# Neighbourhood attention of the first block: the eight turns of a head pair for both heads together, with the next pair's projection chunks between them, and a product with a diagonal in place of scale and transpose

## The chip, the core and the metric

The kernel runs on one core of a Trainium2 chip. The metric is the device time of one execution in microseconds. Engines: PE is TensorE (matmul; PEld its weight loads), DVE is VectorE, ACT is ScalarE, POOL is GpSimd, SP issues most DMAs. Each engine runs its own instructions in order, and they meet at semaphores.

## What is computed

Two transformer blocks on 1024 tokens of 1024 channels in float32. The change is in the first block's mixer: a gated convolution and an attention over eight heads of 64 channels, both from one projection.

```python
z = rms_norm(x, norm1_g) @ w_in                # GLU halves, then q, k, v
conv_out = silu(layer_norm(depthwise_conv31(a * sigmoid(gate)) + bias))
q = rms_norm(q per head, q_norm_g); k = rms_norm(k per head, k_norm_g)
# tokens lie on a 16 x 64 grid; a query sees 8 rows x 16 columns round it
s = q . k * 64**-0.5 + rpb[...]                # per head
attn = softmax(s) @ v
x = x + concat(conv_out, attn) @ w_out         # then the feed-forward and block two
```

## The kernel before

Activations lie with channels on the 128 partitions and tokens along the free dimension. Each large product is made of **units** of 128 output channels: eight **chunks** (one for each 128 input channels) of six matmuls of 512 columns. Inputs and weights are each split in a high and a low fp32r part, and three products (high by high, low by high, high by low) for two halves of the tokens make the six. SP streams a unit's weights to `weight_raw` (two slots), POOL splits them (L386, L388), PE multiplies (`chunk`, L460; matmuls at L465), and DVE takes the result out of PSUM with the per-token scale.

The attention goes over four **pairs** of heads (c = 0 to 3). For each pair PE first makes three units q, k, v. DVE takes them out (L1410, L1412), and q and k are normalised per head: squares on ACT (L1003), a mean per head as a matmul (L488, `head_sum`), a first guess of the inverse root as Ln and Exp on ACT (L937, L939, behind a table load, L933), one refinement and the scaling on DVE (L1319 to L1326, L1422), and the split in high and low (ACT, L1426). Then v is turned by eight transposes (L594) and sixteen **half turns** follow, one head h and one block j of 128 queries each (`na_turn`). In the half turn n PE issues in order:

- `scores(n + 2)` (L559): three matmuls of 384 columns (256 in the first and last block), on 64 partitions, for the head's two or three key blocks;
- `values(n - 1)` (L581): the turned weights times v, one float32 matmul of 128 columns for each key block. A float32 matmul stands as two records;
- `turn(n)` (L572): one transpose of 128 columns for each key block.

DVE adds the bias table to the scores and finds the maximum (L1441), ACT takes the exponent with its sum (L1034), DVE the reciprocal (L1450), ACT multiplies by it (L1041), PE transposes, ACT copies to `probs_t` (L917). DVE also works on the 124 **taps** of the depthwise convolution, one pass over 1024 columns each (L1372, `conv`), some of them between the other steps: one follows each reciprocal. With c = 3 the taps are over, and the LayerNorm of the convolution is done between the steps (L1455 to L1507), with SiLU at the eleventh half turn (L1051). Then the output projection begins (L611); its first unit waits for each mix chunk's split (`mix_hi`, `mix_lo`).

The order of everything is written out by hand, engine by engine.

## Time and profile before

| | us |
|---|---|
| median of 3 runs | 2814.89 |
| lowest, highest | 2813.39, 2815.87 |
| the profiled execution | 2817.12 |
| its span, first to last instruction | 2815.1 |

The profiled execution is 2.2 us above the median, and 2.0 us of it lie outside the span. The span is read as stretches of time: the units of the first gated part end near 119.5 us, the four pairs lie between there and 529.5 us, where the output projection begins, and all that follows is untouched by the change. "Granted clock" is TensorE's, as a share of full speed (2.4 GHz); it is at 1.00 or 0.50, and a mean over a stretch can be in between.

### The profile page before, as it was taken

How to read it: one execution, taken by the hardware profiler on the slowest of the kernel's cores; microseconds unless marked ns; L12 is line 12 of the kernel's file. 1: busy time of each engine (PE TensorE's matmuls, PEld its weight loads, DVE VectorE, ACT ScalarE, POOL GpSimd, SP SyncE). 2: the span in 40 equal slices, each digit the busy share in tenths (PEclk: the TensorE clock that was granted, in tenths of full speed). 3: DMA queues.
4: the chain of work that ended last, by engine and by line, in shares of the span. 5: the costliest groups of instructions: out<-in, count | busy, mean ns of one | idle time of the engine just before them, and what ended most of it. 6: DMA issues, size and time to landing. Idle time of an engine off the chain costs nothing.

```text
span 2815.1 us, 27456 instructions
## 1 busy us (share of the span) xinstructions
PE 2605.6 (93%) x10996; PEld 2033.9 (72%) x10996; DVE 1245.3 (44%) x1214; ACT 679.0 (24%) x908; POOL 932.0 (33%) x431
## 2 busy tenths in 40 slices
PE   8898998999999999999988888796999999999979
PEld 6666665678888888887765555374788888888857
DVE  7967755243222222222835555646522222222465
ACT  3143334421000100000216546612310001100241
POOL 4311102144444444443521111025334343343353
PEclk9968767799999999999989889698999999999989
DMA  3101000211111111111300000021111111111112
GB/s 125 46 22 29 17 13 8 90 45 46 48 50 45 52 45 52 45 52 31 116 30 15 16 15 8 0 105 30 38 53 45 52 45 52 45 52 45 53 37 82
DMA packets 47789, 126.38 MB, mean 45 GB/s; under 512 B 19104, under 2 KB 19104, under 8 KB 45664
## 3 DMA queue, kind: packets, MB, share of 16 engines
q1 hardware_dynamic: 40592, 124.90, 13.8%
q10 hardware_dynamic: 7120, 0.40, 0.2%
q8 instruction: 55, 0.90, 0.1%
q14 instruction: 22, 0.18, 0.0%
HBM read 116.68 MB, written 8.79 MB: 45 GB/s over the span
## 4 chain that ended last, share of the span: by engine, by line
PE 76%; DVE 9%; issue 5%; ACT 5%; POOL 2%; ACTq 1%; DMA 1%; SPq 0%; POOLq 0%; DVEq 0%
PE ps L465 62%; PE ps L811 3%; PE ps L581 3%; PE ps L559 2%; DVE conv_out L1372 2%; PE ps L572 2%; ACTq L972 1%; PE ps L743 1%; PE ps L488 1%; POOL weight_hi L386 1%; ACT sb_e L1160 1%; ACT sb_e L1158 1%; POOL weight_lo L388 1%; POOL branch_out L425 1%; ACT sb_e L1162 1%
## 5 line engine op out<-in xcount | busy, mean ns | idle before, releaser
L386 POOL TENSOR_TENSOR weight_hi<-weight_raw,zero_col 128x1024 fp32r<-128x1024 f32 (+1 forms) x195 | 373.7, 1916 | 1822.2 <-PE ps L465 1479.7
L465 PE MATMUL ps<-input_lo,weight_hi 128*128 128x512 f32 x2032 | 637.9, 396 | 17.7 <-DVE gate_lo L1790 15.9
L465 PE MATMUL ps<-input_hi,weight_hi 128*128 128x512 f32 x1904 | 604.5, 399 | 49.2 <-DVE input_lo L1339 35.4
L465 PE MATMUL ps<-input_hi,weight_lo 128*128 128x512 f32 x1904 | 592.3, 393 | 0.0
L388 POOL TENSOR_TENSOR weight_lo<-weight_raw,weight_hi 128x1024 fp32r<-128x1024 f32 (+1 forms) x195 | 503.5, 2582 | 15.3
L465 PEld LDWEIGHTS ps<-input_hi,weight_hi 128*128 128x128 f32 x1904 | 361.3, 191 | 141.5 <-issue 43.0
L465 PEld LDWEIGHTS ps<-input_lo,weight_hi 128*128 128x128 f32 x2032 | 388.4, 191 | 103.3 <-ACT input_lo L917 12.7
L465 PEld LDWEIGHTS ps<-input_hi,weight_lo 128*128 128x128 f32 x1904 | 362.5, 190 | 76.6
L465 PE MATMUL ps<-hidden_hi,weight_hi 128*128 128x512 f32 x864 | 231.2, 389 | 3.4 <-DVE hidden_lo L1553 3.4
L465 PE MATMUL ps<-hidden_lo,weight_hi 128*128 128x512 f32 x864 | 231.8, 390 | 0.0
L465 PE MATMUL ps<-hidden_hi,weight_lo 128*128 128x512 f32 x864 | 231.5, 390 | 0.0
L465 PEld LDWEIGHTS ps<-hidden_hi,weight_hi 128*128 128x128 f32 x864 | 162.1, 188 | 37.5 <-issue 3.8
L465 PEld LDWEIGHTS ps<-hidden_hi,weight_lo 128*128 128x128 f32 x864 | 162.7, 188 | 33.9
L465 PEld LDWEIGHTS ps<-hidden_lo,weight_hi 128*128 128x128 f32 x864 | 162.7, 188 | 33.9
L1372 DVE SCALAR_TENSOR_TENSOR conv_out<-glu_padded,taps_sb,conv_out 128x1024 f32<-128x1024 f32 x120 | 178.8, 1490 | 2.4
L1099 ACT ACTIVATE work_b<-work_a 128x1024 f32<-128x1024 f32 x32 | 34.0, 1061 | 563.9 <-DVE work_a L1548 563.9
L1562 DVE TENSOR_TENSOR branch_out<-ps,branch_out 128x1024 f32<-128x1024 f32 x56 | 65.9, 1219 | 204.8 <-PE ps L465 204.8
L1562 DVE TENSOR_TENSOR residual<-ps,residual 128x1024 f32<-128x1024 f32 x48 | 56.5, 1218 | 155.2 <-PE ps L465 155.2
L1548 DVE SCALAR_TENSOR_TENSOR work_a<-ps,token_scale 128x1024 f32<-128x1024 f32 x32 | 39.2, 1225 | 177.0 <-PE ps L465 168.0
L1540 DVE TENSOR_TENSOR work_c<-ps,token_scale 128x1024 f32<-128x1024 f32 x22 | 26.9, 1224 | 202.6 <-PE ps L465 202.6
L1097 ACT ACTIVATE work_b<-work_a 128x1024 f32<-128x1024 f32 x22 | 23.4, 1061 | 378.8 <-DVE work_a L1537 378.8
L1666 DVE SCALAR_TENSOR_TENSOR sb_e<-ps,sb_e 128x1024 f32<-128x1024 f32 (+3 forms) x48 | 46.0, 958 | 129.3 <-ACT sb_e L1162 129.3
(238 smaller groups left out, 2877.5 us busy)
## 6 DMA issues: line engine op xcount, KB each, us to landing
weight_raw<-w_ff SPq DMA_DIRECT2D x40, 512.0 KB, 3.5
weight_raw<-w_mlp SPq DMA_DIRECT2D x32, 512.0 KB, 3.5
weight_raw<-w_mlpd SPq DMA_DIRECT2D x32, 512.0 KB, 3.5
weight_raw<-w_ffd SPq DMA_DIRECT2D x20, 512.0 KB, 3.5
weight_raw<-w_out SPq DMA_DIRECT2D x16, 512.0 KB, 3.6
weight_raw<-w_in SPq DMA_DIRECT2D x16, 512.0 KB, 3.5
residual<-x SPq DMA_DIRECT2D x7, 1024.0 KB, 9.3
weight_raw<-w_qkv SPq DMA_DIRECT2D x12, 512.0 KB, 3.7
```

The source lines that it names most:

```text
L386: pool_.tensor_tensor(WH[:, slot, 0:width], raw, ZERO[:].to_broadcast([P, width]), ALU.add).then_inc(s["w_hi"], 1)
L388: pool_.tensor_tensor(WL[:, slot, 0:width], raw, WH[:, slot, 0:width].bitcast(f32), ALU.subtract).then_inc(s["w_split"], 1)
L465: last = mm(PS[:, b + 2 * c + h, :], w[:, slot, k * n + P * c:k * n + P * (c + 1)], a[:, k, h * H2:(h + 1) * H2], start=(k == 0 and step = ...
L559: last = mm(PS[:, 2 + n % 2, 0:nb * QB], q[lo:lo + DH, j * QB:(j + 1) * QB], k_[lo:lo + DH, kb * QB:(kb + nb) * QB], start=(step == 0), st ...
L572: last = nc.tensor.transpose(PS[:, 4 + n % 2, b * P:(b + 1) * P], SB[n % 3][:, b * QB:(b + 1) * QB], IDENT[:])
L581: last = mm(PS[DH * h:DH * (h + 1), 6 + j // 4, (j % 4) * P:(j % 4 + 1) * P], V[:, kb + b, DH * h:DH * (h + 1)], PT[n % 2][:, b, :], start ...
L811: last = mm(PS[:, 7, :], w[:, v % 2, k * P:(k + 1) * P], a[:, k, half * H2:(half + 1) * H2], start=(k == 0 and step == 0), stop=(k == KD - ...
L1099: act_.activation(TB[:], TA[:], ACT.Square).then_inc(s["ff_silu"], 1)
L1372: ins = stt(Y[:, c, :], src, TP[:, c, t:t + 1], Y[:, c, :], ALU.mult, ALU.add)
L1548: stt(TA[:], bank(b), 0.0, RS[:], ALU.max, ALU.mult).then_inc(s["bank_free"], 1)
L1562: ins = tt(dst, src, dst, ALU.add)
L1666: chain(stt(e, PS[:, zb:zb + 2, lo:], 0.0, e, ALU.max, ALU.add))
```

## The change

**PE.** There are eight turns for each pair, each with both heads. `scores` alternates the heads (partitions 0 to 63 and 64 to 127) within each of its three products, and `values` alternates them too. The next pair's q, k and v chunks are set between a turn's steps by the table `BESIDE` (chunk numbers 0 to 23, and the four half means m0 to m3), in one PSUM bank pair. A weight block is turned by a float32 matmul with a diagonal matrix of reciprocal sums (`diag_share`), where a transpose stood. For the last pair, `scores` is preceded by four matmuls of 512 columns whose result is overwritten. The output projection's first two units are interleaved and take the mix chunks in the order 4, 5, 6, 0, 1, 2, 3, 7.

**ACT.** The multiplication by the reciprocal is gone. The head norms go by halves, with a square of the guess (`guess_squared`), without table loads between. Norm steps of the next pair stand at the ends of turns. SiLU, the last pair's output and four splits stand behind the last turn.

**DVE.** It makes the diagonal (128x128) after each reciprocal. The norm has three steps of 512 columns for each half where it had three and a scaling. Taps are spread by `TAPS_AT` (26 for each pair); the seven that remain stand in the last pair's first turn.

```diff
+BESIDE = (((0, 1), (2,), (3,), (4,)),
+          ((5,), (6,), (7,), (8, 9)),
+          ((10,), (11,), (12,), (13, 14, "m0")),
+          ((15,), (), (16,), ("m1",)),
+          ((17,), (18,), (), ("m2",)),
+          ((19,), (20,), (), ("m3",)),
+          ((21,), (22,), (), ()),
+          ((23,), (), (), ()))
+TAPS_AT = (5, 4, 5, 2, 3, 3, 1, 3)
+MIX_ORDER = (4, 5, 6, 0, 1, 2, 3, 7)
+        SB = [at(f"scores{i}", [P, 3 * QB], QK0 + 23552 + 1536 * i) for i in range(4)]
+        ST = at("softmax_stats", [P, 3, 16], QK0 + 29696)
+        T2 = at("guess_squared", [P, H2], QK0 + 29888)
+        DG = [at(f"diag_share{h}", [P, P], (QK0 + 31936, C1 + 96)[h]) for h in range(2)]
...
+            def next_piece(c, what):
+                if what in ("m0", "m1", "m2", "m3"):
+                    i = 4 * (c + 1) + int(what[1])
+                    if what == "m0":
+                        pe.wait_ge(s["v_ready"], 2 * c + 2)
+                    else:
+                        pe.wait_ge(s["qk_scaled"], i)
+                    head_mean_square(i, 5)
+                    return
+                j, k = divmod(what, KD)
+                u = U_QKV + 3 * (c + 1) + j
+                if k == 0:
+                    pe.wait_ge(s["w_split"], u + 1)
+                    pe.wait_ge(s["bank_free"], u)
+                last = chunk(u % 2, 0, k)
+                if k == KD - 1:
+                    last.then_inc(s["unit_done"], 1)
...
+                    pe.wait_ge(s["scores_max"], 2 * n)
                 if c == 3:
+                    for i in range(4):
+                        mm(PS[:, 2 + i % 2, :], KH[:, 0:P], QH[:, 0:H2], start=True, stop=True)
+                for q, k_, step in ((QH, KH, 0), (QH, KL, 1), (QL, KH, 2)):
+                    for h in range(2):
+                        lo = DH * h
+                        last = mm(PS[:, 2 + h, 0:nb * QB], q[lo:lo + DH, j * QB:(j + 1) * QB],
                                   k_[lo:lo + DH, kb * QB:(kb + nb) * QB],
                                   start=(step == 0), stop=(step == 2))
-                    last.then_inc(s["scores_done"], 1)
...
-                def turn(n):
-                    pe.wait_ge(s["probs_scaled"], 16 * c + n + 1)
-                    if n >= 2:
-                        pe.wait_ge(s["pt_sb"], 16 * c + n - 1)
-                    elif n == 0:
-                        pe.wait_ge(s["v_ready"], c + 1)
-                    for b in range(key_blocks(na_turn(n)[1])[1]):
-                        last = nc.tensor.transpose(PS[:, 4 + n % 2, b * P:(b + 1) * P],
-                                                   SB[n % 3][:, b * QB:(b + 1) * QB], IDENT[:])
-                    last.then_inc(s["pt_done"], 1)
+            def turn(n, h):
+                pe.wait_ge(s["probs_sum"], 2 * n + h + 1)
+                if n or h:
+                    pe.wait_ge(s["pt_sb"], 2 * n + h)
+                else:
+                    pe.wait_ge(s["qk_scaled"], 4)
+                for b in range(key_blocks(n % CBLOCKS)[1]):
+                    last = mm(PS[:, 4, b * P:(b + 1) * P], SB[2 * (n % 2) + h][:, b * QB:(b + 1) * QB], DG[h][:],
+                              start=True, stop=True)
+                last.then_inc(s["pt_done"], 1)
...
+                pe.wait_ge(s["pt_sb"], 2 * n + 2)
+                for b in range(nb):
+                    for h in range(2):
                         last = mm(PS[DH * h:DH * (h + 1), 6 + j // 4, (j % 4) * P:(j % 4 + 1) * P],
-                                  V[:, kb + b, DH * h:DH * (h + 1)], PT[n % 2][:, b, :],
+                                  V[:, kb + b, DH * h:DH * (h + 1)], PT[h][:, b, :],
                                   start=(b == 0), stop=(b == nb - 1), skip_group_check=True)
-                    last.then_inc(s["pv_done"], 1)
...
-                for n in range(16):
-                    if n < 14:
-                        scores(n + 2)
-                    if n:
-                        values(n - 1)
-                    turn(n)
-                values(15)
+            scores(0)
+            for c in range(4):
+                for j in range(CBLOCKS):
+                    n = CBLOCKS * c + j
+                    def slot(i):
+                        if c < 3:
+                            for what in BESIDE[j][i]:
+                                next_piece(c, what)
+                    turn(n, 0)
+                    if n < 4 * CBLOCKS - 1:
+                        scores(n + 1)
+                    if j == 0:
+                        v_turn(c, 0)
+                    slot(0)
+                    if j == 0:
+                        v_turn(c, 1)
+                    turn(n, 1)
+                    slot(1)
+                    slot(2)
+                    values(n)
+                    slot(3)
+                    if c == 3 and j == 0:
+                        pe.wait_ge(s["bank_free"], U_OUT)
+                        pe.wait_ge(s["ln_in"], 1)
+                        mean(MEAN, LT[0], 0, "ln_mean")
+                    elif c == 3 and j == 3:
+                        pe.wait_ge(s["ln_ssq"], 3)
+                        mean(MEAN, LT[0], 0, "ln_var")
...
+            for i, k in enumerate(MIX_ORDER):
+                pe.wait_ge(s["mix_hi"], i + 1)
+                pe.wait_ge(s["mix_lo"], i + 1)
+                for j in range(2):
+                    if i == 0:
+                        pe.wait_ge(s["w_split"], U_OUT + j + 1)
+                    last = chunk(j, 2 * j, k, first=MIX_ORDER[0], end=MIX_ORDER[-1])
+                    if i == KD - 1:
+                        last.then_inc(s["unit_done"], 1)
...
+            def head_guess(i, b):
+                y0 = (SQ, TC)[i // 2 % 2][:, (i % 2) * H2:(i % 2 + 1) * H2]
+                act.wait_ge(s["qk_m"], i + 1)
+                chain(act_.activation(y0, PS[:, b, :], ACT.Ln, bias=EPSC[:, 0:1]))
+                chain.wait()
+                chain(act_.activation(y0, y0, ACT.Exp, scale=-0.5))
+                chain.wait()
+                if i:
+                    act.wait_ge(s["qk_a"], i)
+                act_.activation(T2[:], y0, ACT.Square).then_inc(s["qk_y0"], 1)
...
+            def exps(n, h):
+                w, m, t = width(n), 2 * (n % CBLOCKS) + h, SB[2 * (n % 2) + h]
+                act.wait_ge(s["scores_max"], 2 * n + h + 1)
+                act_.activation(t[:, 0:w], t[:, 0:w], ACT.Exp, scale=-1.0,
+                                bias=ST[:, 0, m:m + 1], accum_out=ST[:, 1, m:m + 1])\
+                    .then_inc(s["probs_done"], 1)
+            def probs_t(n, h):
+                w = width(n)
+                act.wait_ge(s["pt_done"], 2 * n + h + 1)
+                if n:
+                    act.wait_ge(s["pv_done"], n)
+                copy(PT[h][:, 0:w // QB, :].rearrange("p b q -> p (b q)"), PS[:, 4, 0:w]).then_inc(s["pt_sb"], 1)
...
             for c in range(4):
-                    act.wait_ge(s["probs_sum"], 16 * c + n + 1)
-                    act_.activation(SB[n % 3][:, 0:w], SB[n % 3][:, 0:w], ACT.Identity,
-                                    scale=ST[:, 2, n:n + 1]).then_inc(s["probs_scaled"], 1)
-                    if n < 15:
-                        exps(n + 1)
...
+                for j in range(CBLOCKS):
+                    n = CBLOCKS * c + j
+                    more = n < 4 * CBLOCKS - 1
+                    probs_t(n, 0)
+                    if more:
+                        exps(n + 1, 0)
+                        exps(n + 1, 1)
+                    if j == 0:
+                        if c:
+                            attn_out(c - 1, 0)
+                            attn_out(c - 1, 1)
+                        v_copy(c, 0)
+                        v_copy(c, 1)
+                    probs_t(n, 1)
+                    if c < 3:
+                        if j == 1:
+                            head_square(c + 1, 0)
+                        elif j == 2:
+                            head_guess(4 * c + 4, 5)
+                        elif j == 3:
+                            head_guess(4 * c + 5, 5)
+                            head_square(c + 1, 1)
+                        elif j == 4:
+                            head_guess(4 * c + 6, 5)
+                        elif j == 5:
+                            head_guess(4 * c + 7, 5)
+                        elif j == 6:
+                            head_hi(c + 1, 0)
+                            head_hi(c + 1, 1)
...
+            def head_norm(i, b):
+                j, half = i // 2 % 2, slice((i % 2) * H2, (i % 2 + 1) * H2)
+                t, y0, ps = (TA, TB)[j][:, half], (SQ, TC)[j][:, half], PS[:, b, :]
+                dve.wait_ge(s["qk_y0"], i + 1)
+                stt(ps, ps, EPS, T2[:], ALU.add, ALU.mult).then_inc(s["qk_a"], 1)
+                dve.wait_ge(s["qk_a"], i + 1)
+                chain(stt(ps, ps, -3.0, y0, ALU.add, ALU.mult))
+                chain.wait()
+                stt(t, ps, GS[:, j:j + 1], t, ALU.mult, ALU.mult).then_inc(s["qk_scaled"], 1)
...
+                if n >= 2:
+                    dve.wait_ge(s["pt_done"], 2 * n - 3 + h)
...
+            def probs(n, h):
+                m = 2 * (n % CBLOCKS) + h
+                dve.wait_ge(s["probs_done"], 2 * n + h + 1)
+                if n:
+                    dve.wait_ge(s["pt_done"], 2 * n - 1 + h)
+                chain(dve_.reciprocal(ST[:, 2, m:m + 1], ST[:, 1, m:m + 1]))
+                chain.wait()
+                ts(DG[h][:], IDENT[:], ST[:, 2, m:m + 1], None, ALU.mult).then_inc(s["probs_sum"], 1)
...
-                scores_in(0)
-                for n in range(16):
-                    if n < 15:
-                        scores_in(n + 1)
-                    probs(n)
+                for j in range(CBLOCKS):
+                    taps_left = TAPS_AT[j] if c < 3 else 0
+                    more = n < 4 * CBLOCKS - 1
+                    if more:
+                        scores_in(n + 1, 0)
+                        scores_in(n + 1, 1)
+                    if taps_left:
+                        conv(1)
+                        taps_left -= 1
+                    if more:
+                        probs(n + 1, 0)
+                        probs(n + 1, 1)
+                        if j == 1:
+                            conv(2)
+                            taps_left -= 2
+                            evac(c + 1, 0, 0)
+                        elif j == 3:
+                            head_norm(4 * c + 4, 5)
+                            evac(c + 1, 1, 0)
+                        elif j in (4, 5, 6):
+                            head_norm(4 * c + 1 + j, 5)
+                        conv(taps_left)
+                        if j == 6:
+                            head_lo(c + 1, 0)
+                            head_lo(c + 1, 1)
+                        elif j == 7:
+                            evac(c + 1, 2, 0)
+                    elif j == 0:
+                        conv(4 * TAPS - tap[0])
+                        chain(tt(LT[0][:], Y[:, 0, :], Y[:, 1, :], ALU.add))
+                        chain.wait()
+                        chain(tt(LT[0][:], LT[0][:], Y[:, 2, :], ALU.add))
+                        chain.wait()
+                        tt(LT[0][:], LT[0][:], Y[:, 3, :], ALU.add).then_inc(s["ln_in"], 1)
+                        mix_lo(4, MIX[4], 0, 0)
...
+                        dve.wait_ge(s["ln_mean"], 2)
...
```

On PE, in the middle of the first pair. Before, two half turns of three key blocks: turn, next scores, values of the half turn before.

```order
L572 MATMUL ps<-identity_60,scores1_85 128x128 x3
L559 MATMUL ps<-k_hi_79,q_hi_77 128x384
L559 MATMUL ps<-k_lo_80,q_hi_77 128x384
L559 MATMUL ps<-k_hi_79,q_lo_78 128x384
L581 MATMUL ps<-probs_t0_82,v_tokens_81 64x128 x3
L572 MATMUL ps<-identity_60,scores2_86 128x128 x3
L559 MATMUL ps<-k_hi_79,q_hi_77 128x384
L559 MATMUL ps<-k_lo_80,q_hi_77 128x384
L559 MATMUL ps<-k_hi_79,q_lo_78 128x384
L581 MATMUL ps<-probs_t1_83,v_tokens_81 64x128 x3
```

After, turn j = 1 of that pair up to the first of two chunks ahead of `values` (L477 is the chunk's matmul, L601 the product with the diagonal, L588 the scores of both heads).

```order
L601 MATMUL ps<-diag_share0_90,scores2_86 128x128 x3
L588 MATMUL ps<-k_hi_79,q_hi_77 128x384 x2
L588 MATMUL ps<-k_lo_80,q_hi_77 128x384 x2
L588 MATMUL ps<-k_hi_79,q_lo_78 128x384 x2
L477 MATMUL ps<-input_hi_50,weight_hi_53 128x512 x2
L477 MATMUL ps<-input_lo_51,weight_hi_53 128x512 x2
L477 MATMUL ps<-input_hi_50,weight_lo_54 128x512 x2
L601 MATMUL ps<-diag_share1_91,scores3_87 128x128 x3
L477 MATMUL ps<-input_hi_50,weight_hi_53 128x512 x2
L477 MATMUL ps<-input_lo_51,weight_hi_53 128x512 x2
L477 MATMUL ps<-input_hi_50,weight_lo_54 128x512 x2
```

What moved: a chunk stands between the two heads' turns, more chunks behind them, and `values` of the same turn behind those.

On DVE, in the middle of the second pair. Before, two half turns.

```order
L1441 ISA scores2_86,softmax_stats_87<-ps,bias_table2_71 128x384
L1441 ISA softmax_stats_87 128x1
L1450 RECIPROCAL softmax_stats_87<-softmax_stats_87 128x1
L1372 SCALAR_TENSOR_TENSOR conv_out_88<-glu_padded_68,taps_sb_64,conv_out_88 128x1024
L1441 ISA scores0_84,softmax_stats_87<-ps,bias_table3_72 128x384
L1441 ISA softmax_stats_87 128x1
L1450 RECIPROCAL softmax_stats_87<-softmax_stats_87 128x1
L1372 SCALAR_TENSOR_TENSOR conv_out_88<-glu_padded_68,taps_sb_64,conv_out_88 128x1024
```

After, the end of turn j = 1 (taking out the next pair's q) and turn j = 2.

```order
L1503 TENSOR_TENSOR work_a_57<-ps,token_scale_55 128x16x8x8
L1470 SCALAR_TENSOR_TENSOR conv_out_92<-glu_padded_68,taps_sb_64,conv_out_92 128x1024
L1533 ISA scores2_86,softmax_stats_88<-ps,bias_table2_71 128x384
L1533 ISA softmax_stats_88 128x1
L1533 ISA scores3_87,softmax_stats_88<-ps,bias_table3_72 128x384
L1533 ISA softmax_stats_88 128x1
L1470 SCALAR_TENSOR_TENSOR conv_out_92<-glu_padded_68,taps_sb_64,conv_out_92 128x1024
L1544 RECIPROCAL softmax_stats_88<-softmax_stats_88 128x1
L1546 TENSOR_SCALAR diag_share0_90<-identity_60,softmax_stats_88 128x128
L1544 RECIPROCAL softmax_stats_88<-softmax_stats_88 128x1
L1546 TENSOR_SCALAR diag_share1_91<-identity_60,softmax_stats_88 128x128
L1470 SCALAR_TENSOR_TENSOR conv_out_92<-glu_padded_68,taps_sb_64,conv_out_92 128x1024 x4
```

What moved: the two heads' scores are read together, one tap stands between them and the two reciprocals, and the taking out of the next pair's units stands behind a turn's softmax steps.

## Rows read from the trace of the kernel before

**Rows 1.** The page, part 1: PE, busy time and share of the span.
```profile
PE 2605.6 (93%) x10996; PEld 2033.9 (72%) x10996; DVE 1245.3 (44%) x1214; ACT 679.0 (24%) x908; POOL 932.0 (33%) x431
```

**Rows 2.** Windows: stretch, length, then busy us of each engine, granted clock, DMA.
```profile
164.40:217.00 52.60, 51.07 (x173) 34.92 (x174) 31.72 (x63) 24.09 (x63) 0.00 (x0) 0.50 0.05 13
217.00:265.70 48.70, 41.86 (x169) 31.54 (x168) 37.38 (x39) 14.26 (x20) 13.62 (x6) 0.93 0.11 29
...
418.00:473.00 55.00, 45.36 (x179) 33.06 (x178) 31.21 (x35) 19.42 (x27) 14.55 (x6) 0.90 0.04 10
473.00:529.50 56.50, 48.37 (x166) 32.81 (x165) 23.76 (x54) 40.76 (x76) 0.00 (x0) 0.50 0.00 0
```

**Rows 3.** Timeline of PE, one half turn: start us, length, operation (a run's start to the next).
```profile
287.83 0.90 PE L572 MATMUL ps<-identity,scores 128*128 128x128 f32 x3
288.66 0.69 PE L559 MATMUL ps<-k_hi,q_hi 64*128 64x384 f32 x1
...
289.92 1.54 PE L581 MATMUL ps<-probs_t,v_tokens 128*64 128x128 f32 x6
291.39 0.90 PE L572 MATMUL ps<-identity,scores 128*128 128x128 f32 x3
```

**Rows 4.** Groups of DVE between 125 and 540 us: count, busy us, mean ns, idle before.
```profile
L1372 DVE SCALAR_TENSOR_TENSOR conv_out<-glu_padded,taps_sb,conv_out 128x1024 f32<-128x1024 f32 x90 | 119.5, 1328 | 1.4
L1441 DVE CUSTOM_DVE_ANT_0 scores<-ps,bias_table 128x384 f32<-128x384 f32 x48 | 26.7, 557 | 60.8 <-PE ps L559 60.5
L1450 DVE RECIPROCAL softmax_stats<-softmax_stats 128x1 f32<-128x1 f32 x64 | 10.2, 160 | 11.5 <-ACT scores L1034 11.0
...
L1319 DVE SCALAR_TENSOR_TENSOR ps<-ps,squares 128x512 f32<-128x512 f32 x8 | 5.6, 694 | 3.9 <-ACT squares L939 3.8
...
L1410 DVE TENSOR_TENSOR work_a<-ps,token_scale 128x1024 f32<-128x1024 f32 x4 | 4.9, 1224 | 20.1 <-PE ps L465 20.1
```

**Rows 5.** Groups of ACT in the same stretch.
```profile
L1041 ACT ACTIVATE scores<-scores,softmax_stats 128x384 f32<-128x384 f32 x48 | 29.1, 607 | 0.7 <-DVE softmax_stats L1450 0.7
L1034 ACT ACTIVATE scores<-scores,softmax_stats 128x384 f32<-128x384 f32 x48 | 28.9, 602 | 0.0
L917 ACT ACTIVATE probs_t<-ps 128x384 f32<-128x384 f32 x48 | 23.5, 490 | 81.7 <-PE ps L572 81.7
...
L1034 ACT ACTIVATION_READ_ACCUMULATOR scores<-scores,softmax_stats 128x1 f32 x64 | 12.1, 190 | 0.0
...
L937 ACT ACTIVATE squares<-ps,eps_col 128x512 f32<-128x512 f32 x8 | 5.5, 682 | 3.7 <-PE ps L488 3.7
```

**Rows 6.** Timeline of PE in the second block's attention, at granted clock 1.00.
```profile
1508.42 0.50 PE L743 MATMUL ps<-q_hi,k_hi 64*128 64x512 f32 x2
...
1509.32 0.73 PE L757 MATMUL ps<-sb_softplus_hi,minus_tri_r 128*128 128x512 f32 x2
...
1511.38 0.87 PE L786 MATMUL ps<-sb_weights,v_tokens 128*64 128x384 f32 x4
1512.17 0.50 PE L811 MATMUL ps<-input_hi,weight_hi 128*128 128x512 f32 x1
```

**Rows 7.** Timeline of PE in a dense product: twelve matmuls, two chunks, start to start.
```profile
1399.61 0.62 PE L465 MATMUL ps<-input_hi,weight_hi 128*128 128x512 f32 x2
...
1402.33 0.62 PE L465 MATMUL ps<-input_hi,weight_hi 128*128 128x512 f32 x2
```

**Rows 8.** Windows: the second block's last head pair, columns as in rows 2.
```profile
1740.00:1840.00 100.00, 70.61 (x250) 39.53 (x250) 64.80 (x73) 63.22 (x80) 4.24 (x2) 0.69 0.00 0
```

**Rows 9.** Timeline, how the first pair begins.
```profile
127.10 1.22 DVE L1410 TENSOR_TENSOR work_a<-ps,token_scale 128x1024 f32<-128x1024 f32 x1
...
129.47 3.78 PE L488 MATMUL ps<-squares,mean_head 128*128 128x512 f32 x4 [9.93 <-ACT squares L1003]
...
164.37 0.69 PE L572 MATMUL ps<-identity,scores 128*128 128x128 f32 x2 [1.08 <-ACT scores L1041]
```

**Rows 10.** Timeline of PE: the output projection's start.
```profile
529.50 1.22 PE L465 MATMUL ps<-input_hi,weight_hi 128*128 128x512 f32 x2
```

406 lines of the change are left out of this document (184 added, 222 removed).

## The prediction

> **What bounds the kernel now.** The page's first part says that PE is busy 93% of the span [rows 1], so the end is set by PE and by what PE waits for. I then read the windows over the attention [rows 2]. The reader is to see an alternation: in the stretches with a pair's half turns (164.4 to 217 us; 473 to 529.5 us, and two like the first between) PE is busy nearly all the time, but at a granted clock of 0.50, the lower level (1.2 GHz); in the stretches with unit matmuls it is at 0.93 and 0.90. So the half turns cost what PE's stream costs at half clock. The timeline of one half turn shows it [rows 3]: turn 0.83 us (287.83 to 288.66), scores 1.26 (to 289.92), values 1.47 (to 291.39), in all 3.56 us without a gap. DVE waits 60.5 us for scores in the attention [rows 4] and ACT 81.7 us for turned weights [rows 5]: both have room. A pair costs 217.0 - 164.4 = 52.6 us of half turns and 48.7 us of the next pair's units and norms [rows 2], 101.3 us together.
>
> **The new turn on PE.** At full clock values of one head would take 1.47 / 2 = 0.73 us [rows 3]. The product with the diagonal is the same shape of work, float32, 128 columns, two passes for each block, so I price it by values: 0.73 a head, 1.46 for two. Bounds: the transposes' 0.42 (half of 0.83) below, and twice 0.73 above if the wider weight loads do not hide. Scores of both heads: the second block alternates heads in the same way and takes 0.90 us for six matmuls of 512 columns (1508.42 to 1509.32) [rows 6], by columns 0.68 for 384; one head after the other would be 1.26 [rows 3]. Values of both heads: four passes of 384 columns, the same number of columns as twelve of 128, take 0.79 us (1511.38 to 1512.17) [rows 6]; without overlap 1.47. I take the lower ends, since rows 6 have the same alternation: 1.46 + 0.68 + 0.79 = 2.9 us a turn at full clock, 5.9 at half. A chunk is 2.72 / 2 = 1.36 us at full clock [rows 7]; a pair has 24. PE's work is 24 x 1.36 + 8 x 2.9 = 56 us a pair.
>
> The row shows that three float32 transposes take 0.83 us where six float32 passes take 1.47, a factor of 1.8 [rows 3]. The Trainium skill, "TensorE: Matmul & The Clock Gate", section "Terms", says that transpose mode makes a float32 transpose four times faster, which speaks against this change. By it the product would be 3.3 us at half clock, 0.9 us a head more than I take at full clock, up to 14 us a pair, and the gain would nearly vanish; the trace has the price of the replacing passes, and I go by that.
>
> **The new turn on DVE.** Per pair: 26 taps at 1.33 = 34.6 us; 16 score readings at 0.64 (0.56 and the accumulator read) = 10.2; 16 reciprocals (0.16) with a diagonal. The diagonal (128 columns) is not in the trace; between the one-column reciprocal (0.16) and the 512-column step (0.69) I take 0.25, since a column of the 512-column step costs about 1.3 ns. With the wait between, 16 x 0.45 = 7.2. Three units taken out at 1.22 = 3.7; four norm halves of three 0.69 steps = 8.3; two low parts at 1.2 = 2.5 [rows 4]. Sum 66.5 us. DVE is thus the longer of the two, and a pair cannot go below about 67 us.
>
> **Where they wait for each other.** I walk a middle pair turn by turn; t = 0 is PE's first product of the turn. PE has the next scores ready at 1.8; DVE reads both heads by 3.1, ACT takes the exponents (0.60 + 0.19 each [rows 5]) by 4.8 and `probs_t` of the second head, 0.49, by 5.3; DVE meanwhile does a tap and the first reciprocal, so that PE's next turn may start at 5.2 at the earliest, and `values` at 5.4.
> j = 0: PE has four chunks and v's eight transposes, and the second transposes wait for ACT's queue (two exponents, two output copies, the first v copy): 11.6 us, and 2.6 more at its start for v being taken out.
> j = 1: chunk 8 waits until DVE, behind its softmax steps and three taps, has taken out q: 12.1.
> j = 2: PE full, five chunks: 10.7.
> j = 3: chunk 16 stands ahead of `values` and waits for k, which DVE takes out behind a norm half: 11.8. The next pair's half mean is queued behind both.
> j = 4 and 5: the norm guess on ACT (Ln 0.68, exponent, square, 1.9 in all [rows 5]) delays `probs_t` and `values`: 8.7, 8.2.
> j = 6: 6.6. j = 7: the next pair's scores wait 3.3 us for k's low part: 7.9.
> Sum 80.2 us. The sparse turns (j = 3 to 7) may fall to half clock: the second block's last pair, with PE busy 70.6 of 100 us, has a mean clock of 0.69 [rows 8]. For that and for DVE's slower steps beside POOL's splits I add 2.3: **82.5 us a pair**, 247.5 for three, against 3 x 101.3 = 304 before [rows 2].
>
> **Beginning.** PE waits 9.93 us for the first squares, because four taps stand ahead of the taking out of q (127.10) [rows 9]. In the new order q goes first, about 5 us earlier; table loads fall away and the norm is shorter. I take the first turn at 155 us for 164.4: 9 us gained, between 4 and 12.
>
> **Last pair.** It has no chunks. Its first turn carries seven taps, three additions and a split on DVE (7 x 1.33 + 4 x 1.22 = 14 us), and PE stops for the LayerNorm mean at its end: 24 us. Then turns of 9 (the four products whose result is overwritten add 0.9 at full clock, 1.8 at half), 9.5, 14 (mean of squares), 10, 10, 10 and 3.5, because LayerNorm steps stand between DVE's readings and ACT has four squares and a guess there. At half clock 90 us, at full clock 78; I take 84. SiLU and the last splits, some 13 us on ACT, lie beside the first three chunk pairs of the output projection (8.2 us) and the last `values`; the x loads that wait for the last split have 20 us of unit matmuls over them, so I put both at nothing; with that cover gone they cost 3 us.
>
> **The sum.** Output projection at 155 + 247.5 + 84 = 486.5 us instead of 529.5 [rows 10]: 43 us. All behind it follows unchanged. 2817.1 - 43 = 2774.1 in the profiled execution's terms; the median of the runs is 2.2 lower: **2772 us**.
>
> **Rivals.**
> *Full clock and loose coupling.* The half turns ran at 0.50 while PE was hardly idle (51.07 of 52.6 us), a third of their instructions being transposes [rows 2]; in rows 6 the products with no transposes among them run at 1.00. If dense products hold the clock and DVE runs on without waiting, a pair is 70 us and the last one 75: 155 + 210 + 75 = 440, 89 us gained, 2726 us. The Trainium skill, the same page, section "Part 4: PE-mode transpose", says that transposes do not count as busy for this gate; by it, putting products in their place favours this rival, and the 0.50 in rows 2 agrees. Against it: the walk has PE idle in five of eight turns.
> *Eaten.* The waits at j = 1, 3 and 7 are each 3 us longer, or the product with the diagonal costs its upper bound: a pair 92, the last 95: 155 + 276 + 95 = 526, 3 us gained, 2812 us.
> *Half clock in the pairs too (slower).* If the waits between chunks drop the clock and it stays down, PE needs 24 x 2.72 + 8 x 5.9 = 112 us a pair and the last takes 90: 155 + 336 + 90 = 581, 52 us lost, 2866 us. It decides from a pair of 96 us, that is from a mean clock of about 0.6 over the pair. Against it: unit stretches with gaps ran at 0.90 and 0.93 [rows 2].
> That the heads do not overlap in the new scores and values is not its own case: 8 x (0.58 + 0.68) = 10 us a pair, half of it hidden behind DVE.
>
> **Chances.** Forecast 0.62; full clock 0.20; eaten 0.10 (half of it within 0.2%, the rest on both sides); half clock 0.08. 0.2% is 5.6 us, about what a measurement of this kernel can tell from no change. Faster 0.86, same 0.05, slower 0.09. The range: pairs of 75 to 91 us and a last pair of 75 to 92 give an end of the attention at 455 to 520, 2740 to 2805; a part of the fast rival belongs inside, so 2738 to 2806.
>
> **What would show it.** In the changed profile: first product with a diagonal near 155 us; the same place of the next pairs 80 to 85 us apart; the output projection's start near 486; `scores` of two heads near 0.7 us and the product near 0.75 a head at full clock; granted clock near 1.00 in j = 0 to 2 and mixed later; DVE the busiest for its share, above 0.8 of a pair. Wrong it would be if a pair is under 75 us (the waits are not there) or over 92 (the clock or a queue), or if the last pair exceeds 95.

## The result, and the profile after

The changed kernel takes 2785.69 us (median of four runs, 2783.96 to 2788.02) against 2815.26 us for the kernel before (median of four, 2813.39 to 2815.87): a ratio of 0.9897, 95% interval 0.9879 to 0.9914. It is 29.6 us faster. The forecast was 2772 us, 13.7 us too low, and the range (2738 to 2806) holds the time.

The profiled execution of the changed kernel took 2788.02 us with a span of 2786.3 us, 28.8 us less than the span before. The first fence is the page's first part and then the windows of the first, third and last pair (the second is like the first, at 0.91); their columns are those of [rows 1] and [rows 2].

```profile
PE 2518.1 (90%) x11204; PEld 1981.4 (71%) x11204; DVE 1262.9 (45%) x1270; ACT 644.2 (23%) x855; POOL 937.9 (34%) x431
```
```profile
158.60:245.60 87.00, 69.54 (x394) 52.36 (x394) 65.82 (x109) 29.52 (x67) 15.80 (x6) 0.89 0.09 24
...
332.60:420.00 87.40, 70.45 (x392) 52.63 (x392) 65.48 (x107) 29.99 (x68) 15.83 (x6) 0.90 0.05 14
420.00:493.00 73.00, 41.78 (x248) 29.15 (x248) 46.52 (x85) 28.00 (x60) 0.00 (x0) 0.77 0.00 1
```

The stretches at 0.50 of [rows 2] are gone: PE runs the pairs at a granted clock of 0.89 to 0.91. But it is now idle about a fifth of the time, where it was idle 3% in the half turns before. The next fence has where the pairs and the projection begin, from the timeline of PE: the first product with a diagonal of each pair, then the first product of the output projection, then the first of its third unit.

```profile
158.65 1.22 PE L601 MATMUL ps<-diag_share,scores 128*128 128x128 f32 x4 [2.70 <-DVE diag_share L1546]
...
241.12 0.71 PE L601 MATMUL ps<-diag_share,scores 128*128 128x128 f32 x4
...
327.62 0.71 PE L601 MATMUL ps<-diag_share,scores 128*128 128x128 f32 x4
...
416.12 0.71 PE L601 MATMUL ps<-diag_share,scores 128*128 128x128 f32 x4
...
493.04 0.73 PE L477 MATMUL ps<-input_hi,weight_hi 128*128 128x512 f32 x2
...
524.40 1.19 PE L477 MATMUL ps<-input_hi,weight_hi 128*128 128x512 f32 x2 [8.88 <-POOL weight_lo L399]
```

These rows carry the account in the profiled executions. The projection starts at 493.04 instead of 529.50 [rows 10]: 36.5 us gained. From there to the end of the span it is 2293.3 us, where it was 2285.6: 7.7 us given back, and the last row shows at what, a wait of 8.88 us for the third unit's weights that the kernel before did not have. 36.5 - 7.7 = 28.8 us.

| term | forecast | measured | error, us |
|---|---|---|---|
| first product | 155 | 158.65 | 3.7 late |
| three pairs | 3 x 82.5 = 247.5 | 82.5, 86.5, 88.5 = 257.5 | 10.0 long |
| last pair | 84 | 76.9 | 7.1 short |
| projection starts | 486.5 | 493.04 | 6.5 late |
| behind it | unchanged | 7.7 longer | 7.7 long |

How long a turn of the first pair is can be read from VectorE's reading of the scores (start us, length; there is one such pair of readings in each turn). The turns j = 0 to 7 take 11.3, 11.6, 11.0, 17.3, 8.4, 7.8, 8.2 and 9.7 us; the fence has the two readings around j = 3, 195.10 and 212.40.

```profile
195.10 0.56 DVE L1533 CUSTOM_DVE_ANT_0 scores<-ps,bias_table 128x384 f32<-128x384 f32 x1 [2.71 <-PE ps L588]
...
212.40 0.56 DVE L1533 CUSTOM_DVE_ANT_0 scores<-ps,bias_table 128x384 f32<-128x384 f32 x1 [6.36 <-issue]
```

One turn stands out. The timeline of VectorE, GpSimd and PE there, in order of start:

```profile
196.63 2.46 POOL L397 TENSOR_TENSOR weight_hi<-weight_raw,zero_col 128x1024 fp32r<-128x1024 f32 x1 [13.38 <-PE ps L477]
...
197.57 1.60 DVE L1546 TENSOR_SCALAR diag_share<-identity,softmax_stats 128x128 f32<-128x128 f32 x1
...
199.17 2.34 POOL L399 TENSOR_TENSOR weight_lo<-weight_raw,weight_hi 128x1024 fp32r<-128x1024 f32 x1
199.28 2.31 DVE L1546 TENSOR_SCALAR diag_share<-identity,softmax_stats 128x128 f32<-128x128 f32 x1
201.51 0.68 DVE L1510 SCALAR_TENSOR_TENSOR ps<-ps,guess_squared 128x512 f32<-128x512 f32 x1
...
203.63 1.22 DVE L1503 TENSOR_TENSOR work_b<-ps,token_scale 128x1024 f32<-128x1024 f32 x1
...
204.99 0.77 PE L477 MATMUL ps<-input_hi,weight_hi 128*128 128x512 f32 x1 [7.78 <-DVE work_b L1503]
```

The reader is to see the ends. GpSimd's two splits end at 199.09 and 201.51; the two diagonals end at 199.17 and 201.59. The reading is that they stand still until GpSimd is through: the same instruction takes 0.285 us when it is alone. Behind them on VectorE stand the normalisation and the taking out of k (203.63), and for that PE waits 7.78 us ahead of chunk 16, with the products with V of this turn queued behind it.

### The profile page after: what moved, and what is told of

Same layout as the page of the kernel before. It is cut to its first block, busy times and chain, and to the rows that moved or that the text cites. A ratio compares the mean times of both kernels' runs of the same rounds, so it can differ in the third digit from the quotient of the medians.

```text
span 2786.3 us, 27974 instructions
## 1 busy us (share of the span) xinstructions
PE 2518.1 (90%) x11204; PEld 1981.4 (71%) x11204; DVE 1262.9 (45%) x1270; ACT 644.2 (23%) x855; POOL 937.9 (34%) x431
## 4 chain that ended last, share of the span: by engine, by line
PE 64%; issue 7%; DVE 7%; ACT 5%; POOL 3%; DMA 1%; SPq 0%; POOLq 0%; DVEq 0%; ACTq 0%
PE ps L477 56%; PE ps L868 3%; POOL weight_hi L397 1%; POOL weight_lo L399 1%; DMA weight_raw<-w_out 1%; PE ps L800 1%; ACT sb_e L1257 1%; ACT sb_e L1255 1%; POOL branch_out L436 1%; ACT sb_e L1259 1%; DVE sb_softplus_lo L1798 1%; DVE residual L1905 1%; DVE conv_out L1470 1%; PE ps L843 1%; DVE sb_weights L1813 1%
## 5 line engine op out<-in xcount | busy, mean ns | idle before, releaser
L477 PE MATMUL ps<-input_hi,weight_hi 128*128 128x512 f32 x1904 | 606.6, 400 | 87.9 <-DVE input_lo L1436 37.2
L477 PE MATMUL ps<-input_lo,weight_hi 128*128 128x512 f32 x2032 | 638.6, 396 | 19.2 <-DVE gate_lo L1909 17.4
L477 PE MATMUL ps<-input_hi,weight_lo 128*128 128x512 f32 x1904 | 594.4, 394 | 0.0
L477 PEld LDWEIGHTS ps<-input_hi,weight_hi 128*128 128x128 f32 x1904 | 357.3, 191 | 177.9 <-issue 80.6
L477 PEld LDWEIGHTS ps<-input_lo,weight_hi 128*128 128x128 f32 x2032 | 388.4, 191 | 105.4 <-ACT input_lo L974 13.9
L477 PEld LDWEIGHTS ps<-input_hi,weight_lo 128*128 128x128 f32 x1904 | 362.7, 191 | 77.0
L477 PE MATMUL ps<-hidden_hi,weight_hi 128*128 128x512 f32 x864 | 231.1, 389 | 3.4 <-DVE hidden_lo L1672 3.4
L477 PE MATMUL ps<-hidden_hi,weight_lo 128*128 128x512 f32 x864 | 231.7, 390 | 0.0
L477 PE MATMUL ps<-hidden_lo,weight_hi 128*128 128x512 f32 x864 | 231.7, 390 | 0.0
L477 PEld LDWEIGHTS ps<-hidden_hi,weight_hi 128*128 128x128 f32 x864 | 162.3, 188 | 37.5 <-issue 3.8
L477 PEld LDWEIGHTS ps<-hidden_hi,weight_lo 128*128 128x128 f32 x864 | 162.7, 188 | 33.9
L477 PEld LDWEIGHTS ps<-hidden_lo,weight_hi 128*128 128x128 f32 x864 | 162.6, 188 | 33.8
L1659 DVE TENSOR_TENSOR work_c<-ps,token_scale 128x1024 f32<-128x1024 f32 x22 | 26.9, 1225 | 203.0 <-PE ps L477 203.0
```

What stands on the lines that cost most here:

```text
L477: last = mm(PS[:, b + 2 * c + h, :], w[:, slot, k * n + P * c:k * n + P * (c + 1)], a[:, k, h * H2:(h + 1) * H2], start=(k == first and st ...
```

## The experiments

### Where the clock comes from: products in the old order, transposes in the new

`before_product` is the kernel before with one edit; nothing moves.

```diff
-                        last = nc.tensor.transpose(PS[:, 4 + n % 2, b * P:(b + 1) * P],
-                                                   SB[n % 3][:, b * QB:(b + 1) * QB], IDENT[:])
+                        last = mm(PS[:, 4 + n % 2, b * P:(b + 1) * P],
+                                  SB[n % 3][:, b * QB:(b + 1) * QB], IDENT[:], start=True, stop=True)
```

> The kernel before, with one edit: each of the 176 transposes of softmax weights is a float32 matmul with the identity (six records for three blocks where three stood); all else as before, the multiplication on ACT too. Theory A (transposes hold the clock down): the granted clock in the half turns rises from 0.50 to above 0.85, a half turn of three blocks falls from 3.56 us to about 2.4 (DVE and ACT then set it), some 60 us less in all, about 2755 us. Theory B (what counts is how full the array is, and scores on 64 partitions and values on 64 columns leave it half empty; or the small matmuls as such): the clock stays at 0.50, the half turn grows by 1.47 - 0.83 = 0.64 us to 4.2, about 38 us more, about 2853 us.

Measured: 2778.48 us (2777.46 to 2779.5), ratio 0.9867, interval 0.9848 to 0.9887. This one edit gives 37 us, more than the whole change. The clock did what theory A says, though 37 of its 60 us came. Its windows, over half turns (first and third row) and over units (the second):

```profile
164.00:207.00 43.00, 41.77 (x207) 31.82 (x207) 27.69 (x56) 22.38 (x59) 0.00 (x0) 0.77 0.05 15
207.00:256.00 49.00, 42.07 (x173) 31.69 (x173) 40.38 (x42) 15.07 (x21) 13.62 (x6) 0.93 0.11 30
256.00:300.00 44.00, 42.13 (x250) 32.75 (x251) 38.07 (x67) 24.79 (x64) 0.00 (x0) 1.00 0.06 14
```

The half turns of the second pair, at 0.50 before, run at 1.00, though PE's work grew. The rise itself can be read in the timeline of PE within the first pair; the products (L572) take 1.56 us from start to start of what follows and then 0.86, the products with V (L581) 1.47 and then 0.80:

```profile
181.03 1.54 PE L581 MATMUL ps<-probs_t,v_tokens 128*64 128x128 f32 x6
182.50 1.63 PE L572 MATMUL ps<-identity,scores 128*128 128x128 f32 x6
184.06 0.44 PE L559 MATMUL ps<-k_hi,q_hi 64*128 64x384 f32 x1
...
184.78 0.87 PE L581 MATMUL ps<-probs_t,v_tokens 128*64 128x128 f32 x6
185.58 0.94 PE L572 MATMUL ps<-identity,scores 128*128 128x128 f32 x6
186.44 0.44 PE L559 MATMUL ps<-k_hi,q_hi 64*128 64x384 f32 x1
```

The rise comes late: from 164 to 182.5 us, with PE busy all the time and no transposes of weights, the clock is still 0.50, and in the last pair the half turns are 4.3 us or more apart until 458 us and 2.4 us behind that. Why it takes so long in these two was not tested. So before the change PE was given 1.2 GHz while its stream had no gap [rows 3], and with the transposes replaced the same stream gets 2.4 GHz in the second pair. The Trainium skill, "TensorE: Matmul & The Clock Gate", section "Part 4: PE-mode transpose", says, beside a bf16 transpose, that transposes do not count as busy in the same way for the gate; this pair of kernels agrees with it, 0.50 against 1.00. Whether they count less or not at all it does not tell.

`transpose_unscaled` does the reverse in the changed kernel: it keeps order and diagonals, but TensorE transposes the undivided weights.

```diff
-                    last = mm(PS[:, 4, b * P:(b + 1) * P], SB[2 * (n % 2) + h][:, b * QB:(b + 1) * QB], DG[h][:],
-                              start=True, stop=True)
+                    last = nc.tensor.transpose(PS[:, 4, b * P:(b + 1) * P],
+                                               SB[2 * (n % 2) + h][:, b * QB:(b + 1) * QB], IDENT[:])
```

> The changed kernel with transposes of the softmax weights in place of the products with the diagonal. The diagonals are still made on DVE but not read by PE, so the division by the sums is left out of the computation. Theory A (the product is what keeps the clock up): the clock over a pair falls from 0.89 to below 0.75 and a pair grows from 87 us to 95 or more. Theory B (the chunks of the next pair keep it up): the clock stays within 0.03 of 0.89 and a pair stays at 85 to 88 us; in the last pair, which has no chunks, the clock of 0.77 may fall. PE's turn falls from 0.76 us a head to about 0.45.

Measured: 2779.14 us (2778.34 to 2779.93), ratio 0.987, interval 0.985 to 0.989; mean clock 0.945 against 0.951 for the changed kernel. With chunks of unit products between the turns the transposes do not bring the clock of the first three pairs down (0.90, 0.87 and 0.89); in the last pair, which has no chunks, it is 0.70 for 0.77. They are the cheaper of the two: 6.6 us faster than the changed kernel. Each of the two parts of the change lifts the clock on its own (0.922 to 0.948 and, below, to 0.947); together the second has next to nothing left to lift.

### The wait behind the start of the projection

`early_w_order`: the loads of the third and fourth unit of the output projection are issued ahead of the wait for the last split, and the first two units end one after the other instead of in step.

```diff
-            for j in range(2):
+            for j in range(4):
                 load_unit(U_OUT + j, j % 2, w_out[j])
             sp.wait_ge(s["mix_lo"], 8)
...
-            for i, k in enumerate(MIX_ORDER):
-                for j in range(2):
+            for i, j in [(i, j) for i in range(5) for j in range(2)] + [(i, j) for j in range(2) for i in (5, 6, 7)]:
```

> The changed kernel with two edits: the third and fourth weight units of the output projection are loaded ahead of the wait for the last mix split and of the four x loads, and the first two units' last three mix chunks go unit by unit, so that the first unit ends 4 us earlier. Theory A (the 8.9 us stall of PE at 515.5 us comes from weights queued behind the x loads): the stall goes, 8 to 9 us less, ratio to the kernel before about 0.986, 2777 us. Rival B (POOL's split of 4.2 us after the first unit's end is the rest of it): 1 to 3 us of the stall stay. Rival C (the x loads, now behind nothing, still come too late for the first addition): DVE waits for x and PE for its banks, no gain.

The changed kernel first, SyncE's queue and GpSimd:

```profile
506.10 2.06 SPq L316 DMA_DIRECT2D residual<-x  x4
508.20 20.72 SPq L274 DMA_DIRECT2D weight_raw<-w_out  x4
```
```profile
519.95 1.89 POOL L397 TENSOR_TENSOR weight_hi<-weight_raw,zero_col 128x1024 fp32r<-128x1024 f32 x1 [100.26 <-DMA weight_raw<-w_out]
```

and `early_w_order`, PE at the third unit:

```profile
516.67 0.70 PE L477 MATMUL ps<-input_hi,weight_hi 128*128 128x512 f32 x2 [0.51 <-POOL weight_lo L399]
```

SyncE stands at the wait for the last split until 506.1, then issues four x loads of 1 MB each, and only behind these the third unit's weights, which land at 519.95 (the start of the split that waits for them). PE had nothing to do from 515.5 to 524.40. The same place in the kernel before:

```profile
533.07 1.97 SPq L305 DMA_DIRECT2D residual<-x  x4
```
```profile
546.76 1.89 POOL L386 TENSOR_TENSOR weight_hi<-weight_raw,zero_col 128x1024 fp32r<-128x1024 f32 x1 [85.11 <-DMA weight_raw<-w_out]
```

There PE went on with the first two units without a gap: the wait was there and was just covered. What moved is the last split. Counted from the projection's start it comes at 3.6 us before the change (533.07 - 529.50) and at 13.1 us after it (506.10 - 493.04), since SiLU, the last pair's output and four splits now stand behind the last turn. These 9.5 us pass on to the weights (landed 17.3 and 26.9 us behind the start), while the first two units last 22 us in both. With the two edits, PE waits 0.51 us instead of 8.88. 2777.66 us (2771.52 to 2778.35), ratio 0.9857, interval 0.9841 to 0.9874: 8.0 us less than the changed kernel. This confirms the cause of the last line of the table. What each of the two edits gives was not run singly; with both, GpSimd's split of the third unit starts at 512.16 behind PE's first unit, and no longer behind a load.

### The fourth turn of a pair

`k_first` moves one VectorE instruction; `narrow_splits` takes away what the diagonals stood still for.

```diff
                         elif j == 3:
+                            evac(c + 1, 1, 0)
                             head_norm(4 * c + 4, 5)
-                            evac(c + 1, 1, 0)
```

> The changed kernel with one instruction of VectorE moved: at the fourth turn of a pair the key unit is taken out of PSUM ahead of the query half's normalisation instead of behind it. Theory A (TensorE's 7.8 us wait in that turn is for this eviction, queued behind the normalisation and the two stretched diagonals): the wait falls to 5 us or less, each of the first three pairs is 2 to 4 us shorter, the whole 2776 to 2781. Theory B (VectorE is the bound over the whole pair, the wait only shows where it falls due): the wait turns up at the next taps or at the next eviction, the pairs stay within 1 us of 82.5, 86.5 and 88.5, and the whole at 2783 to 2788.

Measured: 2776.95 us (2776.38 to 2777.53), ratio 0.9862, interval 0.9834 to 0.9891, 8.7 us less. PE's wait falls from 7.78 to 5.66 us, the fourth turn from 17.3 to 14.6, and the pairs are 2.1, 2.2 and 1.9 us shorter. That is 6.2 us; the rest lies outside the three pairs and is not placed. What VectorE does first in that turn counts; it is not bound over the pair as a whole.

```diff
-            splits(4, U_TAIL + 2 * TAIL - 4)
+            splits(4, 8)
+            splits(12, 8, 128)
+            splits(U_OUT, U_TAIL + 2 * TAIL - U_OUT)
```

> The changed kernel with GpSimd's splits of eight weight units (those that run beside the attention pairs from 177 us on) done on 128 of 1024 columns; the other columns keep an older unit's values, so part of the projections is left out. Theory A (the diagonals and some taps take longer on VectorE because GpSimd's splits run beside them): the mean of a diagonal falls from 0.474 us to 0.29 to 0.33, the fourth turn of a pair from 17.3 to 14 us or less, and the whole to 2764 to 2778. Theory B (they are long for another reason, a wait of VectorE that the profile books as the diagonal's duration): the mean stays over 0.42 us, the fourth turn over 16, and the whole within 2781 to 2788. What is left of the pair period under A is the diagonals' own 0.29 us, whose cost is then the difference to the kernel that makes none (2764.5).

Measured: 2768.67 us (2767.27 to 2770.59), ratio 0.984, interval 0.9824 to 0.9857, 17.0 us less than the changed kernel. VectorE and GpSimd at the same place of the first pair:

```profile
194.62 0.97 POOL L397 TENSOR_TENSOR weight_hi<-weight_raw,zero_col 128x128 fp32r<-128x128 f32 x1 [17.69 <-PE ps L479]
...
195.57 0.29 DVE L1548 TENSOR_SCALAR diag_share<-identity,softmax_stats 128x128 f32<-128x128 f32 x1
195.67 0.50 POOL L399 TENSOR_TENSOR weight_lo<-weight_raw,weight_hi 128x128 fp32r<-128x128 f32 x1
...
195.96 0.28 DVE L1548 TENSOR_SCALAR diag_share<-identity,softmax_stats 128x128 f32<-128x128 f32 x1
```

The diagonals take 0.29 and 0.28 us for 1.60 and 2.31, and the fourth turn 12.9 us for 17.3. PE waited for no split within the first three pairs of the changed kernel, so that weights ready earlier are not the reason. The narrow splits free taps too, so the 17.0 us are not the price of the diagonals alone. The third pair is a control within the same run: the units split beside it belong to the output projection and are split in full, and its fourth turn still takes 16.8 us. The mean of a diagonal fell to 0.358 us over the attention, less far than expected, since that pair keeps its stalls. From the reading in the first pair's first turn to the one in the last pair's, 13.6 us are gone, and 3.0 us more ahead of that. Of these, 2.0 us have the same cause: the first narrow split falls not at 177 us but already at 147.41, beside the taking of k's low part, which is one VectorE instruction with two inputs in SBUF. The changed kernel, then `narrow_splits`:

```profile
151.59 3.25 DVE L1518 TENSOR_TENSOR k_lo<-work_b,k_hi 128x1024 fp32r<-128x1024 f32 x1
```
```profile
150.62 1.23 DVE L1520 TENSOR_TENSOR k_lo<-work_b,k_hi 128x1024 fp32r<-128x1024 f32 x1
```

The last 1.1 us lie ahead of 116 us, where the two kernels are the same, and are not explained.

The Trainium skill, "SBUF — State Buffer", section "Who interferes with whom", says that VectorE and GpSimd share a pair of SBUF ports, which one of them holds for a whole instruction while the other is blocked: a VectorE instruction with two inputs in SBUF contends with a GpSimd instruction that reads SBUF, one of a kind that can take both ports, such as a copy or a product with a scalar, can contend, and one with at most one SBUF input outside these modes does not. The rows agree on both sides. The diagonals end 0.08 us after GpSimd; and the taking out of q, which reads PSUM, takes its usual 1.22 us beside a split, while the tap behind it (two inputs in SBUF) takes 1.66 us for 1.28 and the split behind that 3.24 us for 2.34, in the changed kernel's timeline:

```profile
177.47 2.46 POOL L397 TENSOR_TENSOR weight_hi<-weight_raw,zero_col 128x1024 fp32r<-128x1024 f32 x1 [23.72 <-PE ps L477]
178.22 1.22 DVE L1503 TENSOR_TENSOR work_a<-ps,token_scale 128x1024 f32<-128x1024 f32 x1
179.36 1.66 DVE L1470 SCALAR_TENSOR_TENSOR conv_out<-glu_padded,taps_sb,conv_out 128x1024 f32<-128x1024 f32 x1
...
180.01 3.24 POOL L399 TENSOR_TENSOR weight_lo<-weight_raw,weight_hi 128x1024 fp32r<-128x1024 f32 x1
```

### The change taken apart

`act_scale` is the new order alone: the weights are divided on ScalarE as before and transposed, and VectorE makes no diagonals.

```diff
-                chain(dve_.reciprocal(ST[:, 2, m:m + 1], ST[:, 1, m:m + 1]))
-                chain.wait()
-                ts(DG[h][:], IDENT[:], ST[:, 2, m:m + 1], None, ALU.mult).then_inc(s["probs_sum"], 1)
+                dve_.reciprocal(ST[:, 2, m:m + 1], ST[:, 1, m:m + 1]).then_inc(s["probs_sum"], 1)
...
+            def scaled(n, h):
+                w, m, t = width(n), 2 * (n % CBLOCKS) + h, SB[2 * (n % 2) + h]
+                act.wait_ge(s["probs_sum"], 2 * n + h + 1)
+                act_.activation(t[:, 0:w], t[:, 0:w], ACT.Identity, scale=ST[:, 2, m:m + 1])\
+                    .then_inc(s["probs_scaled"], 1)
...
                     probs_t(n, 1)
+                    if more:
+                        scaled(n + 1, 0)
+                        scaled(n + 1, 1)
```

> The changed kernel's order of work, with the softmax weights divided as in the kernel before: ScalarE multiplies them by the reciprocal (0.58 us each, 64 of them) behind its second eviction of a turn, VectorE makes no diagonals, and TensorE transposes instead of multiplying. Everything is computed. Theory A (the pairs ran 86 us instead of the forecast 82.5 because the diagonals sit on VectorE, 30 us of it, and stretch beside GpSimd's splits): the 17.3 us turn falls to about 13, the first three pairs to 79 to 82 us each, and the whole to 2768 to 2776. Theory B (the diagonal's gain is that a turn does not pass through ScalarE a second time): the turns beside few taps grow by 1 us each, the pairs stay at 85 to 88 us, and the whole stays within 2780 to 2792. The clock should not decide: the same order with transposes had 0.945 as its mean against 0.951.

Measured: 2752.86 us (2751.42 to 2754.29), ratio 0.9777, interval 0.9748 to 0.9805. That is 15 us under the lower end of what I expected of theory A: the pairs, reading to reading, are 75.2, 78.0 and 79.4 us (85.4, 87.0 and 88.4 in the changed kernel), and the fourth turn is 12.9. VectorE and PE there:

```profile
195.10 0.36 DVE L1553 RECIPROCAL softmax_stats<-softmax_stats 128x1 f32<-128x1 f32 x2
...
197.49 1.21 DVE L1514 TENSOR_TENSOR work_b<-ps,token_scale 128x1024 f32<-128x1024 f32 x1
```
```profile
198.85 1.19 PE L477 MATMUL ps<-input_hi,weight_hi 128*128 128x512 f32 x2 [4.12 <-DVE work_b L1514]
```

`act_scale_product` is the same with products with the identity.

```diff
-                    last = nc.tensor.transpose(PS[:, 4, b * P:(b + 1) * P],
-                                               SB[2 * (n % 2) + h][:, b * QB:(b + 1) * QB], IDENT[:])
+                    last = mm(PS[:, 4, b * P:(b + 1) * P], SB[2 * (n % 2) + h][:, b * QB:(b + 1) * QB], IDENT[:],
+                              start=True, stop=True)
```

> The kernel of act_scale with products with the identity in place of the transposes, so that it differs from the changed kernel in one thing: the weights are divided on ScalarE and VectorE makes no diagonals. Theory A (in the new order the clock is held up by the chunks between the turns, and the products bring nothing there; what the changed kernel lost is its diagonals): the whole is 2753 to 2762, 0 to 9 us over act_scale, since the products of both heads take 0.4 to 0.5 us more in each of 32 turns than the transposes, and the mean clock is within 0.01 of 0.947. Theory B (products hold the clock up in the new order as they do in the old): the mean clock rises by over 0.01 and the whole falls under 2748.

Measured: 2764.45 us (2762.96 to 2765.95), ratio 0.9818, interval 0.9798 to 0.9838; mean clock 0.949 against 0.947. The product costs 11.6 us, somewhat over the 9 expected, and raises nothing. The five kernels make a table of median us and mean clock:

| | transposes | products | products with diagonals |
|---|---|---|---|
| old order | 2815.3, 0.922 | 2778.5, 0.948 | |
| new order | 2752.9, 0.947 | 2764.5, 0.949 | 2785.7, 0.951 |

So, taken in this order, the change is the sum of three steps: the new order, -62.4 us; transposes into products, +11.6; the division moved into diagonals on VectorE, +21.2. In all -29.6. Taken in another order the steps differ: in the old order the product gives 37 us. The first step holds all else that the change does, such as the norms by halves and the new start of the projection, and these were not taken apart. Of the third, VectorE's diagonals are busy 30.3 us in the changed kernel, where 64 of 0.285 us would be 18.2.

`serial_heads` undoes the alternation of the two heads in the scores and in the products with V.

```diff
-                for q, k_, step in ((QH, KH, 0), (QH, KL, 1), (QL, KH, 2)):
-                    for h in range(2):
-                        lo = DH * h
+                for h in range(2):
+                    lo = DH * h
+                    for q, k_, step in ((QH, KH, 0), (QH, KL, 1), (QL, KH, 2)):
...
-                for b in range(nb):
-                    for h in range(2):
+                for h in range(2):
+                    for b in range(nb):
```

> The changed kernel with the heads one after the other within a turn: all three score products of the first head, then of the second, and the same for the products with V. Theory A (alternating heads run beside each other in the array; 12 records of V's products take 0.88 us for both heads at the full clock, where 6 of one head take 0.87 us): scores go from 0.72 to about 1.4 us for both heads and values from 0.88 to about 1.7, 1.5 us more in each of 32 turns, of which the path takes most: 2810 to 2830. Theory B (a turn is set by the passage through the other engines): the durations grow but the pairs by less than 1 us, and the whole is under 2795.

Measured: 2787.78 us (2785.56 to 2790.01), ratio 0.9901, interval 0.9872 to 0.9929, not to be told from the changed kernel. This is theory B: the passage through the other engines sets a turn. The durations, too, grew far less than expected: the scores of both heads still take 0.72 us (181.53 to 182.25), and their records stand in pairs of one from each head, as if nothing had been reordered; the twelve products with V take 1.07 us for 0.81.

```profile
181.53 0.45 PE L588 MATMUL ps<-k_hi,q_hi 64*128 64x384 f32 x2
181.81 0.34 PE L588 MATMUL ps<-k_lo,q_hi 64*128 64x384 f32 x2
...
182.25 0.73 PE L477 MATMUL ps<-input_hi,weight_hi 128*128 128x512 f32 x2
...
187.27 1.14 PE L618 MATMUL ps<-probs_t,v_tokens 128*64 128x128 f32 x12
188.34 0.74 PE L477 MATMUL ps<-input_hi,weight_hi 128*128 128x512 f32 x2
```

`nofill` leaves out the four matmuls in each turn of the last pair whose result is overwritten.

```diff
-                if c == 3:
-                    for i in range(4):
-                        mm(PS[:, 2 + i % 2, :], KH[:, 0:P], QH[:, 0:H2], start=True, stop=True)
```

> The changed kernel without the four overwritten matmuls ahead of each scores in the last pair (28 matmuls fewer). Theory A (they hold the clock): the last pair's clock falls from 0.77 to about 0.6 and the stretch from its first product to the output projection, 76.9 us now, grows to 80 or more. Theory B (they only cost time): seven times 0.9 to 1.2 us fall away ahead of scores and the stretch is 69 to 72 us; the whole 2779 to 2782 us where the changed kernel is at 2786.

Measured: 2784.62 us (2784.28 to 2784.97), ratio 0.9889, interval 0.9869 to 0.9909. The last pair is 75.8 us (76.9 with them), neither the 80 or more of theory A nor the 69 to 72 of theory B, and its clock 0.71 for 0.77. The four matmuls are worth nothing here; a difference of 1 us lies within the spread of the runs.

### A faster kernel

Two kernels take together what the runs showed. `act_scale_early` is `act_scale` with the loads and order of `early_w_order`; `act_scale_all` adds the eviction of `k_first` and moves taps out of the last pair.

> The kernel of act_scale with the early weight loads and the output projection's order of early_w_order. Theory A: as act_scale, less the whole wait at the third unit, which is 9 us or more there since the projection begins earlier while the loads do not: 2758 to 2768. If the gain of the early loads was tied to the late start of the projection, it is within 3 us of act_scale.

```diff
-TAPS_AT = (5, 4, 5, 2, 3, 3, 1, 3)
+TAPS_AT = (6, 4, 6, 2, 3, 3, 1, 3)
```

> act_scale with all that the single runs pointed to: the early weight loads and the projection's order, the key unit taken out ahead of the normalisation, and one filter tap more in the first and in the third turn of each pair, so that one tap instead of seven is left for the last pair. Expected against act_scale_early (2743.6): 2 us in each of three pairs for the eviction, and up to 6 taps of 1.31 us, 7.9 us, off TensorE's wait in the last pair: 2730 to 2736. If the taps in the first and third turn are not hidden (VectorE waited 5.1 and 2.7 us in those turns), their gain is given back and it is 2737 to 2742.

> The kernel of act_scale_all without the four score-shaped matmuls whose result is overwritten in each turn of the last pair. In the changed kernel leaving them out gave 1 us. If that holds, 1 to 2 us less than act_scale_all; if the clock of the last pair needs them there, since its turns follow one another faster, 1 to 4 us more.

Measured: `act_scale_early` 2743.56 us (2742.34 to 2744.77), ratio 0.9744; `act_scale_all` 2727.36 (2724.7 to 2728.76), ratio 0.9684, interval 0.9668 to 0.9701; without the overwritten matmuls 2721.58 (2719.84 to 2722.28), ratio 0.9667, interval 0.965 to 0.9683. The last is 94 us under the kernel before and 64 under the changed one. `act_scale_early` is 9.3 us under `act_scale`, as expected of the loads; it is under the expected 2758 because `act_scale` is. `act_scale_all` is 16.2 us under `act_scale_early`, where 8 to 14 were expected of the eviction and the taps together; they were not run singly. In the changed kernel the last pair's first turn had this row of VectorE and this of PE:

```profile
427.82 9.20 DVE L1470 SCALAR_TENSOR_TENSOR conv_out<-glu_padded,taps_sb,conv_out 128x1024 f32<-128x1024 f32 x7
```
```profile
440.94 3.75 PE L500 MATMUL ps<-ln_work,mean_all 128*128 128x512 f32 x4 [12.04 <-DVE ln_work L1601]
```

and in `act_scale_all` PE's wait at that place is

```profile
391.15 3.75 PE L500 MATMUL ps<-ln_work,mean_all 128*128 128x512 f32 x4 [0.60 <-DVE ln_work L1608]
```

Between the last two kernels 5.8 us were found, more than the 1 to 2 expected. But the profiled executions, 7.9 us apart, have 3.8 us of it ahead of the first pair, in code that is the same in both; the last pair gives 2.7. The first part is not explained, so what leaving the matmuls out is worth is not settled either, beyond that it does not cost.

## Why the prediction was right or wrong

**The bound.** Right, but for a count: the transposes are a quarter of PE's records in a half turn, 3 of 12 [rows 3], not a third. The half turns did cost what PE's stream costs at half clock, and freeing them of that was the gain: `before_product` gave PE more passes in the same order, the clock of these stretches rose, and 37 us were won. The forecast walked the turns at full clock without naming a cause; that the transposes held it down I wrote only into a rival with a chance of 0.20. Its first half, a clock near full in the pairs, came true (0.89 to 0.91), but in the new order not through the products: with transposes it is 0.87 to 0.90. Its second half, that VectorE runs on without waiting, did not come true.

**The prices on PE.** Right. At full clock a head's product was put at 0.73 us and takes 0.76, the scores of both heads at 0.68 (0.72), the products with V at 0.79 (0.81). The rule of the Trainium skill against the change, four times faster float32 transposes ("TensorE: Matmul & The Clock Gate", section "Terms"), is not what is seen: at full clock three transposes take 0.42 us and six passes 0.76, a factor of 1.8, the one of [rows 3]. Where the rule was right is in its sign: 11.6 us are lost by the product in the new order. I did not ask what the same order would give with transposes.

**The diagonals.** The step that failed first. The prediction says: "between the one-column reciprocal (0.16) and the 512-column step (0.69) I take 0.25": alone it is 0.285 us, so the price was right, but the mean is 0.474 and in the fourth turn it is 1.60 and 2.31. I priced it as so many instructions of such a length and put GpSimd's splits at 2.3 us a pair together with the clock, without looking where the splits fall. They begin as soon as PE is done with a unit, and in j = 3 that is right on the diagonals. I had j = 3 at 11.8 us and it is 17.3 (16.5 and 17.7 in the next two pairs); the first pair's other seven turns, reading to reading, sum to 68.1, where the walk had 68.4. So 2.3 us for all of a pair stood against 5.5 us in this one turn. In the next two pairs the rest is longer too (70.5 and 70.7), in part in the first turn (13.0 and 12.3 for 11.3); no run takes that apart. That the table has the first pair at just the forecast 82.5 is luck of the mark: its first product is followed by the first reading after 2.5 us, and after 5.5 to 5.9 us in the next pairs, where PE also waits for v being taken out (4.15 us at 246.71). From reading to reading it is 85.4 us. `narrow_splits` (12.9 us) and `act_scale` (12.9 us) both show that turn without the stall. What the diagonals cost in all, 21.2 us, is the largest single error of judgement here: the forecast priced the reciprocals and diagonals at 7.2 us of VectorE's time a pair, and never asked what the division costs where it was, on ScalarE, of which it had itself read that it has room.

**Where they wait for each other.** The walk was right for the kind of waits at j = 1 and 3 and for their engine. The wait that grew is the one it named at j = 3, "for k, which DVE takes out behind a norm half", and `k_first` gives 8.7 us by taking k out first.

**Beginning.** 3.7 us late, and the gain was mis-sized in both of its parts. Taking out q first was to give about 5 us and gave 4.1 (123.00 for 127.10). The shorter norm and the table loads that fall away were to give the other 4; from the taking out of q to the first product it was 37.3 us (to 164.37) and is 35.7. The stalls beside GpSimd's splits lie in this stretch, but they are not new. Here are a row of VectorE in the kernel before and three in the changed kernel, the second of them the taking out of q. The taps of the first row of each take 3.6 us longer than alone (1.3 us each); k's low part, 3.25 us now and 1.23 alone, was 2.93 before.

```profile
116.05 7.53 DVE L1372 SCALAR_TENSOR_TENSOR conv_out<-glu_padded,taps_sb,conv_out 128x1024 f32<-128x1024 f32 x3
```
```profile
116.76 6.21 DVE L1470 SCALAR_TENSOR_TENSOR conv_out<-glu_padded,taps_sb,conv_out 128x1024 f32<-128x1024 f32 x2
123.00 1.22 DVE L1503 TENSOR_TENSOR work_a<-ps,token_scale 128x1024 f32<-128x1024 f32 x1
...
138.64 7.35 DVE L1470 SCALAR_TENSOR_TENSOR conv_out<-glu_padded,taps_sb,conv_out 128x1024 f32<-128x1024 f32 x4
```

The row of the kernel before could have been read ahead of the forecast: 7.53 us for three taps. The last row is a candidate for the missing gain: four taps, 5.2 us when alone, stand ahead of k's norm, whose first guess is ready at 142.65 and is used at 146.02. No run takes this apart; `narrow_splits` shows that the stall at k's low part is worth 2.0 us.

**Last pair.** 76.9 us for 84. I had taken the middle between half clock (90) and full clock (78); the mean clock was 0.77, and it hides two halves. The first turn, from the first product to 444.49, was at 0.60 and took 28.4 us for the 24 of the walk; PE stands still there for most of the time. The last four turns, from 472.43 on, were at 0.98 and took 20.6 us, where the walk had 33.5 at half clock. But the clock does not set these four: in `nofill` the same turns are at 0.83 and take 20.1 us. So the waits in the last turns were put too long in the walk at either clock, and the middle between two clocks came near by luck. Why they are shorter was not looked into. The stop for the LayerNorm mean behind the seven taps was there, 12.04 us.

**Behind the projection's start.** The second step that failed: "the x loads that wait for the last split have 20 us of unit matmuls over them, so I put both at nothing; with that cover gone they cost 3 us". I looked at who waits for the x loads and not at what is queued behind them on SyncE, the third unit's weights. The change puts SiLU and the last splits behind the last turn, and so the last split 9.5 us further behind the projection's start. It cost 8.88 us of waiting, 7.7 in all; the 3 us that I named as the risk were for the x loads alone.

**The sum.** Errors of 3.7 + 10.0 - 7.1 + 7.7 = 14.3 us in the profiled execution, 13.7 in the medians. The sign and the range held; of the forecast gain of 43 us two thirds came. It is luck that the last pair was 7.1 us short: without that the error had been 21 us. The largest error, the pairs, comes in the main from GpSimd's splits. Neither "eaten" nor "half clock" came about: no pair is over 88.5 us, and the clock over the first three pairs did not fall below 0.89.

## What to carry to other kernels

When two edits of a change cure the same trouble, price each on top of the other: here the new order alone gives 62 us, the product alone 37, and both together less than the first. Before work is moved to an engine that waits much of its time, lay it beside what GpSimd does at that very time, and place it by its turn and not by a mean. And when work is put behind the end of a stretch, ask of every queue that feeds what follows whether its next load stands behind a wait for that work.

## What the hardware showed that was not expected

- TensorE's clock stayed at 0.50 through 52.6 us in which it was busy 51.07 and had three float32 transposes in each half turn. When these became products of twice the passes it was 1.00 in the second pair; in the first it was still 0.50 for the first 18.5 us. With unit products between the turns the same transposes left it at 0.87 to 0.90 (`transpose_unscaled`).
- A VectorE instruction of 0.285 us took up to 2.31 us beside GpSimd's splits, and ended 0.08 us after them. Taps and splits hold up one another: 1.28 us becomes 1.66, two taps 6.21 for 2.6, and a split 3.24 for 2.34. This shows in a profile as a longer duration, not as idle time.
- The score products of the two heads, on different halves of the rows, take 0.72 us together in either order of issue, and one head alone took 0.72 as well (184.06 to 184.78 in `before_product`).
